# A PEER expert layer on one core: gate matrix stored by block, expert tables read in runs of 8 KB

## What is computed

```python
qry = (xf @ w_query).reshape(T, 8, 2, 128)
sa = einsum('thd,nd->thn', qry[:, :, 0], sub_keys_a)      # 128 scores a head
sb = einsum('thd,nd->thn', qry[:, :, 1], sub_keys_b)
va, ia = top_k(sa, 16); vb, ib = top_k(sb, 16)
cand = va[..., :, None] + vb[..., None, :]
cand_idx = ia[..., :, None] * 128 + ib[..., None, :]      # expert number, 0 .. 16383
top_s, pos = top_k(cand, 16)
experts = take_along_axis(cand_idx, pos)                  # 8 x 16 experts a token
gates = softmax(top_s)
act = gelu(einsum('tkd,td->tk', expert_u[experts], xf))
out = einsum('tk,tkd->td', gates * act, expert_v[experts])
```

## Time and profile before

| | us |
|---|---|
| runs of the kernel before | 4109.92, 4118.97, 4119.53 |
| their median | 4118.97 |
| span of the profiled execution | 4056.0 |
| PE busy in it | 3497.1 (86%) |
| DVE busy | 2775.1 (68%) |
| POOL busy | 1556.6 (38%) |
| ACT busy | 907.0 (22%) |

### The profile page before, as it was taken

How to read it: one execution, slowest core, us unless ns; L and a number is a source line. 1 busy time by engine, 2 the same in 40 slices (tenths; PEclk the granted TensorE clock), 3 DMA queues, 4 the chain that set the end, 5 groups by cost and what they waited for, 6 DMA issues and landing times.

```text
span 4056.0 us, 39947 instructions
## 1 busy us (share of the span) xinstructions
PE 3497.1 (86%) x13253; PEld 1966.8 (48%) x13253; DVE 2775.1 (68%) x5292; ACT 907.0 (22%) x1917; POOL 1556.6 (38%) x1400
## 2 busy tenths in 40 slices
PE   7999958888765688985899889899999898989995
PEld 3444435555552588885444444444444444444442
DVE  1222234566442378887698888988888988987787
ACT  0111115566321025546100111101110111101110
POOL 0000000000165000000565666666666666667675
PEclk9999966998877799998899999999999899999997
DMA  8222032110264456563998999999999999999997
GB/s 302 88 90 89 34 118 74 48 44 32 49 190 142 169 204 255 209 249 132 348 360 307 395 376 388 360 373 391 386 386 335 393 386 384 358 376 403 397 400 278
DMA packets 345757, 1044.35 MB, mean 257 GB/s; under 512 B 32160, under 2 KB 82640, under 8 KB 341392
## 3 DMA queue, kind: packets, MB, share of 16 engines
q0 software_dynamic: 184336, 667.00, 43.9%
q1 hardware_dynamic: 161216, 374.80, 25.4%
HBM read 974.27 MB, written 67.14 MB: 257 GB/s over the span
## 4 chain that ended last, share of the span: by engine, by line
DVE 20%; DMA 14%; POOL 8%; DVEq 5%; issue 4%; PE 1%; SPq 0%; ACT 0%; POOLq 0%
DMA pick_v<-in_expert_v,ids 13%; DVE acc L2486 10%; DVE e_junk L2470 6%; POOL pick_u L2296 4%; DVEq L2481 4%; POOL pick_v L2304 4%; PE psH L2356 1%; DVE e_away L1771 1%; DVE e_found L1774 1%; DVE e_W L2435 1%; DMA e_u<-in_expert_u 1%; DVEq L1737 0%; DVE e_spare L1732 0%; DVE e_ia L1731 0%; DVE e_va L1734 0%
## 5 line engine op out<-in xcount | busy, mean ns | idle before, releaser
L2356 PE MATMUL psH<-XT,e_uT 128*128 128x512 f32 x2048 | 966.0, 613 | 122.3 <-ACT e_uT L2393 122.3
L2369 PE MATMUL psY<-e_v,e_W 128*128 128x512 f32 x2048 | 891.0, 597 | 19.3 <-DVE e_W L2435 19.3
L2486 DVE SCALAR_TENSOR_TENSOR acc<-pick_v,pick_w,acc 128x1024 f32<-128x1024 f32 x571 | 733.5, 1285 | 231.8 <-DMA pick_v<-in_expert_v,ids 189.6
L2296 POOL DMA_INDIRECT pick_u<-in_expert_u,ids x576 | 712.1, 1236 | 393.6 <-DVE pick_dot L2470 259.0
L2304 POOL DMA_INDIRECT pick_v<-in_expert_v,ids x576 | 658.7, 1144 | 281.5 <-issue 161.3
L2470 DVE CUSTOM_DVE_ANT_0 e_junk<-pick_u,x_rows 128x1024 bf16<-128x1024 f32 x576 | 702.9, 1220 | 26.2 <-DMA pick_u<-in_expert_u,ids 14.0
L2369 PEld LDWEIGHTS psY<-e_v,e_W 128*128 128x128 f32 x2048 | 392.1, 192 | 515.6 <-issue 487.9
L2356 PEld LDWEIGHTS psH<-XT,e_uT 128*128 128x128 f32 x2048 | 380.2, 197 | 510.6 <-issue 369.7
L385 PE MATMUL ps_p<-w_in_sb,hT 128*128 128x512 f32 x1008 | 441.0, 597 | 0.0
L385 PEld LDWEIGHTS ps_p<-w_in_sb,hT 128*128 128x128 f32 x1008 | 190.9, 191 | 231.8 <-issue 231.7
L2393 ACT ACTIVATE e_uT<-psU 128x512 f32<-128x512 f32 x256 | 149.0, 594 | 638.0 <-PE psU L2348 637.9
(11 more groups left out here) (453 smaller groups left out, 3888.1 us busy)
## 6 DMA issues: line engine op xcount, KB each, us to landing
w_query_sb<-in_w_query SPq DMA_DIRECT2D x36, 2048.0 KB, 8.1
e_u<-in_expert_u SPq DMA_DIRECT2D x128, 512.0 KB, 7.2
e_v<-in_expert_v SPq DMA_DIRECT2D x128, 512.0 KB, 11.1
G_d<-G_stage SPq DMA_DIRECT2D x16, 2048.0 KB, 12.0
e_g<-G_d SPq DMA_DIRECT2D x16, 2048.0 KB, 26.1
w_ada<-in_w_ada POOLq DMA_DIRECT2D x16, 1024.0 KB, 10.1
w_in_sb<-in_w_in SPq DMA_DIRECT2D x7, 2048.0 KB, 19.3
pick_u<-in_expert_u,ids POOLq DMA_INDIRECT x576, 8.6
```

Source lines behind the costliest of these rows:

```text
L2296: pool.indirect_dma_start(gu[:, i % NGU, :], None, io["expert_u"][0], bass.IndirectOffsetOnAxis(ids[:, q % 2, j:j + 1], 0)).then_inc(pu_in ...
L2356: m = pe.matmul(psH[a % 2][:, :], uT[:, a % 2, j, :], XT[:, j, :], start=j == 0, stop=j == KD - 1)
L2369: m = pe.matmul(psY[i % NY][:, :], W[:, (b * NBK + t) % NW, k * P:(k + 1) * P], v[:, t, half_cols(half)], start=t == 0, stop=t == NBK - 1)
L2486: dve.scalar_tensor_tensor(out=sums_q, in0=gv[:, i % NGV, :], scalar=wgt[:, m % 2, o:o + 1], in1=sums_q, op0=ALU.mult, op1=ALU.add).then_i ...
```

## The change

The tile of experts becomes "b fixed, all a": partition a holds row 128 a + b. Neighbouring tiles then hold neighbouring rows, and two tiles lie side by side in memory on every partition: 8 KB. Each SP load of u or v takes two tiles. `e_u` gets a fourth buffer. The gate matrix is laid out as [a, block, 32-token group, tile, token], so the gates of a block are 16 KB in one piece for each partition, and a store writes sixteen pieces of 1 KB for each partition where it wrote one of 16 KB. The operands of `psG` are swapped so that a stands on the partitions.

```diff
-        G_d = dram("G_d", (TD // HT, P, NK, HT))
+        G_d = dram("G_d", (P, NK // NBK, TD // HT, NBK, HT))
...
-                sp.dma_start(G_d[q], gs[:, q % NS_, :, :]).then_inc(g_stored[q % NS_], 16)
+                sp.dma_start(G_d[:, :, q, :, :].rearrange("p m n t -> p m (n t)"), gs[:, q % NS_, :, :].rearrange("p (m n) t -> p m (n t)", n=NBK)).then_inc(g_stored[q % NS_], 16)
...
-                    m = pe.matmul(psG[:, i % 2, t, :], ob[:, i % NO, t, :], oa[:, i % NO, t, :], start=True, stop=True)
+                    m = pe.matmul(psG[:, i % 2, t, :], oa[:, i % NO, t, :], ob[:, i % NO, t, :], start=True, stop=True)
...
-    NBK, NU, NW, NY = 8, 3, 9, 4
+    NU, NW, NY, VT = 4, 9, 4, 2
...
-        u_rows = io["expert_u"][0].rearrange("(a b) d -> a b d", b=P)
-        v_rows = io["expert_v"][0].rearrange("(a b) d -> a b d", b=P)
+        u_rows = io["expert_u"][0].rearrange("(b a) d -> b a d", b=P)
+        v_rows = io["expert_v"][0].rearrange("(b a) d -> b a d", b=P)
...
-            def load_v(b, t):
-                if b >= 1 and t == 0:
+            def load_v(b, n):
+                if b >= 1 and n == 0:
                     sp.wait_ge(y_out, UNITS * b)
-                sp.dma_start(v[:, t, :], v_rows[b * NBK + t]).then_inc(v_in[t], 16)
+                sp.dma_start(v[:, n * VT:(n + 1) * VT, :], v_rows[:, b * NBK + n * VT:b * NBK + (n + 1) * VT, :]).then_inc(v_in[n], 16)
...
-                sp.dma_start(g[:, :, :, :], G_d[:, :, b * NBK:(b + 1) * NBK, :].rearrange("q b a t -> b q a t")).then_inc(g_in, 16)
+                sp.dma_start(g[:, :, :, :], G_d[:, b]).then_inc(g_in, 16)
...
-                if a >= NU:
-                    sp.wait_ge(u_turned, 2 * (a - NU + 1))
-                sp.dma_start(u[:, a % NU, :], u_rows[a]).then_inc(u_in[a % NU], 16)
+                if a % 2 == 0:
+                    if a >= NU:
+                        sp.wait_ge(u_turned, 2 * (a - NU + 2))
+                    sp.dma_start(u[:, a % NU:a % NU + 2, :], u_rows[:, a:a + 2, :]).then_inc(u_in[a % NU // 2], 16)
...
-                if b >= 1 and t == NU:
+                if b >= 1 and t == 3:
                     load_gates(b)
                 if 4 <= t < NBK:
-                    load_v(b, 2 * (t - 4))
-                    load_v(b, 2 * (t - 4) + 1)
+                    load_v(b, t - 4)
```

More of the change, by code:

```diff
@@ L49 @@
 HT = 32
+NBK = 8
 D0, D1 = 4, 8
@@ L2203, in apply @@
         set_up = sem("e_setup")
-        u_in, g_in, v_in = [sem(f"e_u_in{i}") for i in range(NU)], sem("e_g_in"), [sem(f"e_v_in{i}") for i in range(NBK)]
+        u_in, g_in, v_in = [sem(f"e_u_in{i}") for i in range(NU // 2)], sem("e_g_in"), [sem(f"e_v_in{i}") for i in range(NBK // VT)]
         u_turned, u_kept, h_out, h_act, weighed, y_out, y_added = (sem(f"e_{n}") for n in ("u_turned", "u_kept", "h_out", "h_act", "weighed", "y_out", "y_added"))
@@ L2341, in turn @@
             def turn(a, half):
-                if half == 0:
-                    pe.wait_ge(u_in[a % NU], 16 * (a // NU + 1))
+                if half == 0 and a % 2 == 0:
+                    pe.wait_ge(u_in[a % NU // 2], 16 * (a // NU + 1))
                 if a >= 1:
@@ L2367, in sums @@
                         pe.wait_ge(weighed, b * NBK + t + 1)
-                        pe.wait_ge(v_in[t], 16 * (b + 1))
+                        if t % VT == 0:
+                            pe.wait_ge(v_in[t // VT], 16 * (b + 1))
                     m = pe.matmul(psY[i % NY][:, :], W[:, (b * NBK + t) % NW, k * P:(k + 1) * P], v[:, t, half_cols(half)], start=t == 0, stop=t == NBK - 1)
```

## The result

Twenty runs of each kernel, taken together: 4112.95 us before (4102.35 to 4126.08), 4121.86 after (4112.71 to 4129.99), ratio 1.0017 with the interval 1.0009 to 1.0025. By the prediction's own bound of 0.3% that is no measurable change, on the slow side of one. The 22 us of gain did not come.

A forecast was written before the change was run, and what follows sets the result against it. The prediction took `apply` as bound by DMA, with DVE and PE close behind. Its terms, -18 - 10 + 10 - 5 + 1 = -22 us, took 4119 us to 4097, in a range of 4050 to 4145.

The forecast's parts named there:

- Gates and tables, -28 us: Cheaper packets in gate and table loads of `apply`: 18 us and 10 us saved, all counted as time.
- Burst, +10 us: Denser gate loads in `apply` hold up gathers; DVE's landed rows mostly cover it, costing 0.6 us a block.
- The rival "slower": Gate burst empties DVE's buffers: 4.6 us a block, 4161 us if all blocks are hit, 4124 if half; chance 0.22.
- v loads, nothing: Paired v loads in `apply` come in denser bursts, but as many gathers pass in two tiles: no time taken.
- SP queue, nothing: Waits of paired u loads on the SP queue: PE keeps enough lead, so no time taken.
- Start, -5 us: At the start of `apply`, tiles 0 and 1 load ahead of the gates: 5 us of PE's 9.6 us wait saved.
- Routing, +1 us: Gate stores in 1 KB pieces: 15 hide behind stage buffers, the last costs 1 us.
- The rival "nothing measurable": No measurable change, by the 512 KB pitch or by burst and saving in balance: chance 0.26.
- The 63 us: Gap between the profiled span of 4056.0 us and the runs' median 4118.97, left unchanged in the forecast.
- Pitch rival: Table rows 512 KB apart slow 8 KB packets; 40 ns more is 41 us, gain gone; within the 0.26 for nothing measurable.
- Larger gain: Bursts ending earlier let DVE's buffers fill, waits shrink by a third, 61 us: 4054 us; chance 0.10.

The follow-up runs named there:

- tables alone: Changed kernel with the gate layout, store and load of the kernel before: ratio 0.9989 to the kernel before.
- gates in 4 KB pieces at once: Changed kernel with each block's gate load cut into four loads issued together: ratio 0.9984 to the kernel before.
- paced pieces: Changed kernel with each gate load cut into four, later ones waiting for the previous block's sums: ratio 0.9977 to the kernel before.
- the spread order: v loads spread over a block's length, gates in four paced pieces: changed kernel 0.9908, again 0.9914; kernel before, tile by tile, 0.9953; all against the kernel before.
- the repeat: The changed kernel run once more, unaltered, beside the cut gate loads: ratio 1.0005 to the kernel before.
- the mapping alone: Kernel before with the new mapping of rows to partitions and psG operands swapped, single-tile loads, old gate layout: ratio 1.0005.
- a fifth buffer: Kernel before with v loads spread, gates paced and a fifth buffer of pick_v: ratio 0.9945, against 0.9953 without that buffer.
- the last pair: Changed kernel with v spread and gates paced, repeated, against the kernel before in that order: 14 blocks 1800.0 and 1806.2 us.

## Why the prediction was wrong

**Gates and tables, -28 us.** The engine time came as worked out: 28.7 us over 14 blocks. The step that failed is the next one, "I let all of it count because DMA is the largest term and its share is 1.00 over the block". Five comparisons over 14 blocks without a 16 KB burst price it in the steady state: tables alone -3.6 us for 12 us of engine time saved, all with gates in 4 KB pieces at once -1.5 for 26, the same with paced pieces +3.3 for 27, the whole change in the spread order -0.2 for 20 and, repeated, -6.2 for 21. Each is within the scatter of a single profile; their mean is some 2 us shorter for some 21 us saved. Forecast were 25 on 14 blocks. The share told how busy the engines were, not that they set the pace. It simply falls when work is taken out, to 0.96. What a block waits for is single landings of gathers. That a bulk load which uses less engine time in one stretch doesn't bring forward a gather in another is how I read this; no run tests it by itself.

**Burst, +10 us.** The mechanism is the one described: 16 KB packets against 4 KB packets, one for one, a hole of some 6 us in the gathers. The step that failed here is its price, 0.6 us a block. I sized it by DVE's wait in the same window before, 0.6 us in one block: a window with little waiting shows how DVE fares under the old load and doesn't show how much of its stock is spare. Measured are 3.3 - 0.9 = 2.4 us a block in those windows, and against the 4 KB pieces at the same place 14 to 23 us over the 14 blocks in the profiles, 10 us by the medians of the runs. The rival "slower" named this cause with 4.6 us a block and a threshold of four blocks in ten. Its price was twice too high, and its end of 4161 us was far off. Yet its mechanism is what takes the gain of the start away.

**v loads, nothing.** Right for the change itself: in the 36 us after the first v load the mean wait of DVE is 5.3 us a block against 6.1. But these loads cost the kernel before and the changed one alike; spreading them alone took 16 us off the changed kernel.

**SP queue, nothing.** Right: PE waits for u nowhere in the 14 blocks.

**Start, -5 us.** Right in kind, but sized at half of the 10.4 us that came. PE's wait for u of tile 1 behind the gate load is gone; tile 1 is turned within the same run as tile 0 in the timeline of PE:

```profile
1990.12 1.94 PE L2349 MATMUL psU<-e_ident,e_u 128*128 128x128 f32 x8 [22.68 <-DMA e_u<-in_expert_u]
...
1996.49 3.60 PE L2357 MATMUL psH<-XT,e_uT 128*128 128x512 f32 x8
```

I had held it to half on the argument that the first weighing waits for the first gathers. The chains in order of time (start, duration) say otherwise. Before, the chain enters `apply` through the load of tile 1, which was issued behind the gates, and goes on through PE's products:

```profile
1924.40 23.23 DMA e_u<-in_expert_u
1948.79 5.84 PE psH L2356 x8
```

With the gates' layout alone that landing takes 7 us less, and the start gains 8:

```profile
1919.40 16.50 DMA e_u<-in_expert_u
```

With the table pairs alone tile 1 is early, but tiles 2 and 3 stand behind the long gate load, PE waits 6.9 us for them, and the start gains 2. With the whole change the chain no longer passes through PE there. It goes through a gathered row of `expert_u` that lands 33 us after the start of `apply`. Gathers are the limit that I had named, but I had put it at the first of them, 22 us after the start:

```profile
1994.51 19.07 DMA pick_u<-in_expert_u,ids
```

**Routing, +1 us.** 2.2 us, with gate stores landing in 13.0 us (median) where they took 12.0.

**Sum as measured.** About -10 (start), +2 (routing), -6 to +3 (engine time saved), +10 to +23 (burst), which is -4 to +18 us; `apply` and routing together show 11.4 + 2.2 in the profile pair, the medians 8.9, and those of the repeat 4.3. The rival "nothing measurable" had burst and saving in balance. Its outcome came, by another balance: the burst against a start gain of twice the forecast, with the saving near nothing. That these two cancel is chance.

**The 63 us.** They were carried through the sum as what lies around the span. In every run whose span is known that is only some 2 us (4126.42 us for the changed kernel's span of 4124.7); the rest is the later begin of routing. It shifts both kernels alike and leaves the forecast of 22 us as it is.

**Pitch rival.** It gives a like result, no measurable change, from a cause that is absent: with the mapping alone the ratio is 1.0005, with every packet of the tables at 512 KB pitch, the hardware queue's share is the same 21.2%, and the 8 KB packet takes 313 ns. By the 3% of the Trainium skill (DMA: Bandwidth & Descriptors, Latency and other measured facts) it would have been some 325 ns, an estimate; this kernel's trace does not show it. The page's figure is for copies between tensors in HBM with 16 KiB for each partition, where these loads have 4 and 8 KB. The 16 KB runs of the gates have a pitch of 256 KB and were not tried with a padded one, but their 614 ns a packet, beside the 621 of the stores, show no such loss.

**Larger gain.** It asked whether bursts that end earlier let the buffers fill. They do the opposite. That fewer waits of DVE are worth time fits the runs, and it needed the loads' order: on the kernel before 163.9 down to 143.2 us of waits, 20 us of the 14 blocks.

**Open.** What holds the block at 129.0 us in the spread order, where DVE is busy 113 and still waits 10 for gathers at a DMA share of 0.98 to 0.99, and a fifth buffer adds nothing that these runs can tell. And how much of the 6 us of the last pair is engine time saved, as the scatter of single profiles is as large.

## What to carry to other kernels

Larger runs make a bulk load cheaper and at the same time denser: on a path where another queue fetches small pieces just in time, look first at how long those fetches are held up, and cut or pace the load to that. A DMA share near 1.00 is no proof that less DMA work is less time; ask for which landing the engines wait and whether the saved work stands before it. Before laying out data anew, try the order and the pieces in which the loads that are there are issued: here it gave 0.47% without a byte moved elsewhere, and each added wait must be followed down its queue, as the v load behind the gate load shows.

## What was not expected of the hardware

The gathers' own packets did not get cheaper when the bulk loads did: their queue took 0.767 x 1826.15 = 1400.7 us before and 0.766 x 1847.64 = 1415.3 after for the same 147 thousand packets, 1% more. And where both queues had work, their packets alternated from 1 KB (1926 gathers against 2161) to 16 KB (85 against 85), so that a queue's share of the time went with the length of its packets: 29.2% for the hardware queue with pieces of 1 KB, 48.8% with 4 KB, 81.5% with 16 KB.
